# Two-layer encoder on one core: h split ahead of the squares, first three projection groups in three PSUM banks, GpSimd's constants ahead of the bias

## The reference

```python
def rms_norm(x, g):
    xf = x.astype(jnp.float32)
    y = xf * lax.rsqrt(jnp.mean(xf * xf, axis=-1, keepdims=True) + EPS)
    return (y * g.astype(jnp.float32)).astype(x.dtype)

# layer 0: h = rms_norm(x, mix_norm[0]); x = x + neighbourhood_attention(h, ...)
qkv = jnp.einsum('bsd,de->bse', h, w_qkv)       # 1024 -> 3072, 16 heads of 64
s = jnp.einsum('bchd,brckhd->bhcrk', q_r, k_win)
s = s + bias[None]                              # relative bias rpb, gathered by position
p = jax.nn.softmax(s...)
```

## Time and profile before

| | |
|---|---|
| median of three runs | 1189.57 us |
| the profiled execution: its own time, its span | 1191.49 us, 1189.8 us |
| PE busy | 1158.5 us, 97% of the span |
| DVE busy | 644.4 us, 54% |
| ACT busy | 473.6 us, 40% |
| POOL busy | 129.4 us, 11% |
| mean granted TensorE clock | 0.992 |

### The profile page before, as it was taken

How to read it: one execution, slowest core, us unless ns; L and a number is a source line. 1 busy time by engine, 2 the same in 40 slices (tenths; PEclk the granted TensorE clock), 3 DMA queues, 4 the chain that set the end, 5 groups by cost and what they waited for, 6 DMA issues and landing times.

```text
span 1189.8 us, 17258 instructions
## 1 busy us (share of the span) xinstructions
PE 1158.5 (97%) x5940; PEld 953.3 (80%) x5940; DVE 644.4 (54%) x1075; ACT 473.6 (40%) x809; POOL 129.4 (11%) x243
## 2 busy tenths in 40 slices
PE   6899999999999999999999999999999999999995
PEld 4788888877888888888888777787888888888883
DVE  7567677666443224544435888967544233544334
ACT  6444455544342213433233566645443212433221
POOL 4733432050000000000000122100000000000000
PEclk9899999999999999999999999999999999999997
DMA  7322221143222323232232122112222323232321
GB/s 207 99 75 83 68 69 67 51 118 106 94 100 90 103 90 105 88 106 89 88 106 89 50 63 62 33 70 88 93 101 90 105 88 106 88 106 89 106 88 71
DMA packets 35698, 106.74 MB, mean 90 GB/s; under 512 B 8096, under 2 KB 8368, under 8 KB 35664
## 3 DMA queue, kind: packets, MB, share of 16 engines
q1 hardware_dynamic: 30528, 98.98, 25.0%
q0 software_dynamic: 4992, 7.29, 2.8%
q10 hardware_dynamic: 144, 0.02, 0.0%
HBM read 102.92 MB, written 3.34 MB: 89 GB/s over the span
## 4 chain that ended last, share of the span: by engine, by line
PE 92%; DVE 3%; issue 1%; ACT 1%; SPq 1%; POOL 1%; DMA 1%; DVEq 0%; ACTq 0%; POOLq 0%
PE acc L342 26%; PE acc L344 25%; PE acc L343 25%; PE s_ps L342 3%; PE s_ps L343 2%; PE s_ps L344 2%; PE pt_ps L535 2%; PE o_ps L342 1%; PE o_ps L344 1%; PE o_ps L343 1%; PE pt_ps L427 1%; SPq L242 1%; DVE rstd L873 1%; DVE w_lo L851 1%; PE misc_ps L404 1%
## 5 line engine op out<-in xcount | busy, mean ns | idle before, releaser
L632 ACT CAST w_hi<-w_raw 128x1024 fp32r<-128x1024 f32 x180 | 189.1, 1051 | 441.9 <-PE acc L344 430.6
L342 PE MATMUL acc<-h_hi,w_hi 128*128 128x512 f32 x800 | 322.7, 403 | 10.5 <-DVE sqsum L868 9.9
L344 PE MATMUL acc<-h_hi,w_lo 128*128 128x512 f32 x800 | 312.9, 391 | 0.0
L343 PE MATMUL acc<-h_lo,w_hi 128*128 128x512 f32 x800 | 312.8, 391 | 0.0
L851 DVE TENSOR_TENSOR w_lo<-w_raw,w_hi 128x1024 fp32r<-128x1024 f32 x180 | 220.2, 1223 | 147.7 <-ACT w_hi L632 147.6
L342 PE MATMUL acc<-u_hi,w_hi 128*128 128x512 f32 x608 | 238.2, 392 | 0.9 <-DVE w_lo L851 0.9
L344 PE MATMUL acc<-u_hi,w_lo 128*128 128x512 f32 x608 | 236.7, 389 | 0.0
L343 PE MATMUL acc<-u_lo,w_hi 128*128 128x512 f32 x608 | 236.6, 389 | 0.0
L342 PEld LDWEIGHTS acc<-h_hi,w_hi 128*128 128x128 f32 x800 | 150.9, 189 | 50.7 <-issue 17.3
L344 PEld LDWEIGHTS acc<-h_hi,w_lo 128*128 128x128 f32 x800 | 151.0, 189 | 32.0
L343 PEld LDWEIGHTS acc<-h_lo,w_hi 128*128 128x128 f32 x800 | 151.3, 189 | 29.0 <-issue 1.0
(11 more groups left out here) (83 smaller groups left out, 1145.8 us busy)
## 6 DMA issues: line engine op xcount, KB each, us to landing
w_raw<-in_wstream SPq DMA_DIRECT2D x180, 512.0 KB, 3.3
bias_pairs<-rpb_shifted POOLq DMA_DIRECT2D x64, 48.0 KB, 3.1
bias_pairs<-t_shifted POOLq DMA_DIRECT2D x64, 48.0 KB, 2.5
x_res<-in_xT SPq DMA_DIRECT2D x8, 256.0 KB, 4.5
out_y<-x_res SPq DMA_DIRECT2D x8, 256.0 KB, 2.1
t_shifted<-vT POOLq DMA_DIRECT2D x16, 31.0 KB, 1.8
rpb_shifted<-rpb_pad POOLq DMA_DIRECT2D x8, 45.0 KB, 5.2
rpb_shifted<-rpb_pad SPq DMA_DIRECT2D x8, 45.0 KB, 8.1
```

What stands on the lines that cost most here:

```text
L342: nc.tensor.matmul(dst, a[0], b[0], start=start, stop=False)
L343: nc.tensor.matmul(dst, a[0], b[1], start=False, stop=False)
L344: return nc.tensor.matmul(dst, a[1], b[0], start=False, stop=stop)
L632: nc.scalar.copy(w_hi[:, c.odd, :], w_raw[:, c.odd, :]).then_inc(w_hi_made, 1)
```

## The change

ACT and DVE make all eight pieces of h first, and the squares and their sums after them (`first_high`, `first_low`, `first_square`, `first_sum`). PE does groups 0, 1 and 2 in acc0, acc1 and half of `pt_ps`, with `statistics` between groups 1 and 2 (`first_tiles`), so none of the three waits for a bank to be taken out. DVE takes all three results after the reciprocal, and chunk 3 is split ahead of it. On POOL the loads of `sink`, `table` and `onehot_sb` stand before the stores of the bias, and the load of the second pair's bias stands behind the masking of the first pair's. Of the 16 stores SP issues 4 instead of 8, POOL 12 instead of 8.

```diff
@@ SP
-            for c in range(0, QC, 2):
+            for c in range(0, QC, 4):
                 sp.dma_start(rpb_dram[c], rpb_pad[:, :, QC - 1 - c:QC - 1 - c + BIASC]).then_inc(rpb_stored, 16)
@@ POOL
             pool.dma_start(mask[:], na_mask).then_inc(consts_landed, 16)
+            pool.dma_start(sink[:], sinks.partition_broadcast(P)).then_inc(consts_landed, 16)
+            pool.dma_start(table[:], rel_table).then_inc(table_landed, 16)
+            pool.dma_start(onehot_sb[:], onehot).then_inc(table_landed, 16)
             pool.wait_ge(rpb_landed, 16)
-            for c in range(1, QC, 2):
+            for c in range(QC):
+                if c % 4 == 0:
+                    continue
...
             load_na_bias(At(0))
-            load_na_bias(At(1))
-            pool.dma_start(sink[:], sinks.partition_broadcast(P)).then_inc(consts_landed, 16)
-            pool.dma_start(table[:], rel_table).then_inc(table_landed, 16)
-            pool.dma_start(onehot_sb[:], onehot).then_inc(table_landed, 16)
             pool.wait_ge(consts_landed, 16 * 2)
             masked_bias(At(0), 0)
             masked_bias(At(0), 1)
+            load_na_bias(At(1))
@@ PE
+            def first_tiles():
+                for n in range(3):
+                    pe.wait_ge(w_split, CH_NA + n + 1)
+                    bank = acc[n][:] if n < 2 else first_v
+                    for k in ALL:
+                        if n == 0:
+                            pe.wait_ge(first_split, k + 1)
+                        b = slice(k * P, (k + 1) * P)
+                        ins = product(bank, (w_hi[:, n % 2, b], w_lo[:, n % 2, b]), h_tile(k), k == 0, k == KT - 1)
+                    ins.then_inc(w_used, 1)
+                    if n == 1:
+                        statistics(0)
@@ ACT
             for k in range(KT):
-                prepare_x(0, At(k), lambda: act.wait_ge(x_landed[k], 16))
+                first_high(k)
                 if k == 5:
                     split_weights(At(1))
-            na_step(At(0), attend=False)
+            for k in range(KT):
+                first_square(k)
+                if k == 5:
+                    split_weights(At(2))
+            load_sqrt()
+            split_weights(At(3))
+            deviation(0)
+            tile_high(At(GR_NA), At(TI_NA), u_hi[:, 8, :], order=(in_tiles, by_tile))
+            tile_high(At(GR_NA + 1), At(TI_NA + 1), k_hi[:, 0, :], order=(by_column, tokens))
+            split_weights(At(4))
@@ DVE
             for k in range(KT):
-                finish_x(0, At(k))
+                first_low(k)
                 if k == 5:
                     split_weights(At(1))
-            na_step(At(0), attend=False)
+            for k in range(KT):
+                first_sum(k)
+                if k == 5:
+                    split_weights(At(2))
+            split_weights(At(3))
+            reciprocal_deviation(0)
+            scale_tile(At(CH_NA), At(GR_NA), At(TI_NA), HD ** -0.5)
+            scale_tile(At(CH_NA + 1), At(GR_NA + 1), At(TI_NA + 1), 1.0)
+            tile_low(At(TI_NA), u_lo[:, 8, :], u_hi[:, 8, :], (in_tiles, by_tile))
+            tile_low(At(TI_NA + 1), k_lo[:, 0, :], k_hi[:, 0, :], (by_column, tokens))
+            dve.wait_ge(w_used, CH_NA + 3)
+            nc.vector.scalar_tensor_tensor(out=by_column(vT[:, :]), in0=tokens(flat(pt_ps[:, 0:QT, :])), scalar=1.0,
+                                           in1=tokens(rstd[:]), op0=ALU.mult, op1=ALU.mult).then_inc(acc_taken, 1)
+            split_weights(At(4))
```

More of the change, by code:

```diff
@@ L165, in encoder @@
         squared, tile_hi, tile_split = sem("squared"), sem("tile_hi"), sem("tile_split")
+        first_hi, first_split = sem("first_hi"), sem("first_split")
         x_prepared, h_split, sq_cleared = sem("x_prepared"), sem("h_split"), sem("sq_cleared")
@@ L300, in place_sinks @@
                 nc.gpsimd.tensor_copy(sw_nsink[:, pair.odd, :], nsink[:, heads]).then_inc(sinks_placed, 1)
-            pool.wait_ge(rpb_stored, 16 * QC // 2)
-            pool.wait_ge(rpb_stored_odd, 16 * QC // 2)
+            pool.wait_ge(rpb_stored, 16 * QC // 4)
+            pool.wait_ge(rpb_stored_odd, 16 * QC // 4 * 3)
             load_na_bias(At(0))
-            load_na_bias(At(1))
-            pool.dma_start(sink[:], sinks.partition_broadcast(P)).then_inc(consts_landed, 16)
-            pool.dma_start(table[:], rel_table).then_inc(table_landed, 16)
-            pool.dma_start(onehot_sb[:], onehot).then_inc(table_landed, 16)
             pool.wait_ge(consts_landed, 16 * 2)
@@ L392, in statistics @@
                 nc.tensor.matmul(flat(misc_ps[:]), ones[:], sqsum[:], start=True, stop=True).then_inc(stat_done, 1)
+            first_v = flat(pt_ps[:, 0:QT, :])
+            def first_tiles():
[10 more added lines that the diff above has]
+                        statistics(0)
             def part_after_norm(c, g, n):
@@ L458, in dense_part @@
                 def dense_part(n):
-                    if dense and m.a == 0 and n == 0:
-                        part_after_norm(c, g, 0)
-                    elif dense:
+                    if dense:
                         part(c + n, g + n, h_tile, ALL)
@@ L587, in _ @@
             pe.wait_ge(ident_made, 1)
-            na_step(At(0), attend=False)
+            first_tiles()
             na_step(At(1))
@@ L644, in prepare_x, with first_high, first_square @@
                                      ACT.Square).then_inc(x_prepared, 1)
+            def first_high(k):
+                act.wait_ge(x_landed[k], 16)
+                act.wait_ge(gain_landed, 16)
+                nc.scalar.activation(h_hi[:, k, :], x[:, k, :], ACT.Copy, scale=gain[:, k:k + 1]).then_inc(first_hi, 1)
+            def first_square(k):
+                if k >= 2:
+                    act.wait_ge(h_split, k - 1)
+                nc.scalar.activation(probs[:, SEQ * (k % 2):SEQ * (k % 2 + 1)], x[:, k, :],
+                                     ACT.Square).then_inc(x_prepared, 1)
             def gain_of(n, k):
@@ L703, in na_step @@
                 if dense:
-                    if m.a == 0:
-                        load_sqrt()
-                        deviation(0)
                     split_weights(c + 2)
@@ L868, in finish_x, with first_low, first_sum @@
                 nc.vector.tensor_tensor(sqsum[:], sqsum[:], probs[:, SEQ * k.odd:SEQ * (k.odd + 1)],
+                                        ALU.add).then_inc(h_split, 1)
+            def first_low(k):
+                dve.wait_ge(first_hi, k + 1)
+                nc.vector.scalar_tensor_tensor(out=h_lo[:, k, :], in0=x[:, k, :], scalar=gain[:, k:k + 1],
+                                               in1=f32(h_hi[:, k, :]), op0=ALU.mult,
+                                               op1=ALU.subtract).then_inc(first_split, 1)
+            def first_sum(k):
+                dve.wait_ge(x_prepared, k + 1)
+                if k == 0:
+                    dve.wait_ge(sq_cleared, 1)
+                else:
+                    dve.wait_ge(h_split, k)
+                nc.vector.tensor_tensor(sqsum[:], sqsum[:], probs[:, SEQ * (k % 2):SEQ * (k % 2 + 1)],
                                         ALU.add).then_inc(h_split, 1)
@@ L943, in na_step @@
                 if dense:
-                    if m.a == 0:
-                        reciprocal_deviation(0)
                     e = m * 2 + TI_NA
```

## The result

The changed kernel takes 1191.19 us, the median of 20 runs (1189.04 to 1197.02), against 1188.58 for the kernel before, measured beside it (20 runs, 1186.42 to 1192.34). The ratio is 1.0024, with a 95% interval of 1.0015 to 1.0034. A gain of 4.3 us was forecast, and it is 2.6 us slower, outside the range that I gave.

A forecast was written before the change was run, and what follows sets the result against it. PE's 3.86 us idle before the transposes, from POOL's order and SP's queue, was taken as the bound. Transposes 1.0 us earlier plus 3.3 us of clock loss not repeated gave 4.3: 1189.57 to 1185.3 us, range 1180.5 to 1189.5.

The forecast's parts named there:

- The three constants: POOL's front: issuing these loads takes 0.57 us each of 3.18 us idle before the stores, so costs nothing.
- I put it at 20, against a need at 21.4: Front: chunk 3, requested at about 13 behind four SP stores, lands at 20, before its split is needed at 21.4.
- rival C: Front: DVE's chain ends 3 to 4 us late, as when chunk 3 lands after 21.4; 1189.5 us, chance 0.1.
- Rival D: POOL's queue: stores crawl, last lands at 33; 1195 us; decides only from a last store past 30.5; chance 0.05.
- The clock: PE: the clock falls in the new 3.2 us idle at 27.6, losing 3.3 us there instead of later.
- Case B: The forecast itself: PE's clock falls in the new idle; gain 4.3 us, 1185.3 us, chance 0.5.
- The base: Whole kernel: gain reckoned against the profiled 1191.49 us, then taken from the median of 1189.57, including 3.3 us not lost again.
- case A: PE: the clock holds in the new idle ahead of the scores; gain 7.4 us, 1182.2 us, chance 0.35.
- The bias: POOL and SP: last store lands at 19.5, masking done at 29.4, or 31.1 with the latest store, ahead of need.
- The rule of the Trainium skill that I weighed: Bias stores: all issuers share 16 engines, so the last store stays at 22.4; mask at 32.6, still before 33.1.

The follow-up runs named there:

- e10: The changed kernel again, unaltered, for a second profile: 1192.81 us, ratio 1.0025 to before.
- e3: The changed kernel with the loads of sink, table and onehot issued behind POOL's stores: 1189.82 us, ratio 0.9997 to before.
- e2: The changed kernel's new front with POOL and SP as in the kernel before: 1192.09 us, ratio 1.0022 to before.
- e6: The changed kernel with only the load of sink moved behind the stores: 1190.34 us, ratio 1.0015 to before.
- e12: e6 with a stand-in load, 128 rows of 64 bytes from different places, where the changed kernel loads sink: 1191.28 us, ratio 1.0018 to before.
- e5: e3 with chunk 3's split moved behind the values' scaling on DVE and two rounded tiles on ACT: 1187.32 us, ratio 0.9984 to before.
- e11: The changed kernel with a second load of sink right behind the first: 1192.84 us, ratio 1.0031 to before.
- e9: The kernel before with the load of sink alone moved ahead of the stores: 1190.69 us, ratio 1.0005 to before.
- e1: The front of before with the changed kernel's whole POOL and SP part, constants first: 1187.70 us, ratio 0.9981 to before.
- e4: The front of before with the changed POOL and SP part, but constants behind the stores: 1186.48 us, ratio 0.9970 to before.
- e7: e4 with the stores divided as before, eight by SP and eight by POOL: 1186.78 us, ratio 0.9983 to before.
- e8: e5 with four squares and sums between h's pieces, chunk 2 split after sums, statistics inside group 1, chunk 3 split before values' scaling: 1184.85 us, ratio 0.9974.

## Why the prediction was wrong

- **"The three constants take 0.57 each of the 3.18 us that POOL idles before the stores, so nothing."** This step failed first. I priced the issue on POOL and not the transfer on the engines that x is using. `sink`, 8 KB, delays x by 2.4 (k = 3) to 3.1 us (k = 7). In the new front all eight sums stand behind the last piece of x, and that carried 3.0 to the last sum, 2.9 to the reciprocal and 3.2 to the scores.
- **"I put it at 20, against a need at 21.4" (chunk 3).** It landed at 23.0 in the profile of after, 25.2 in e10, 23.5 in e3. This is rival C's mechanism, to which I gave 0.1. In the profile of after it is hidden behind the late x (ACT reaches the split at 24.26); in e2, e3, e6 and e12 it is waited for. The first error covers this one, which is why mending the first alone (e3, e6, e12) brings the scores only 1.2 to 2.7 us forward where x comes 2.8 to 3.1 earlier. I had the row of one chunk that was requested at another time, not what lay ahead of this one: four stores of SP and twelve of POOL. In e3 SP's last store landed at 18.4, and this is what the DMA engines did from 17 to 19 us:

```profile
DMA packets 158, 0.15 MB, mean 75 GB/s; under 512 B 110, under 2 KB 110, under 8 KB 158
q0 software_dynamic: 85, 0.14, 102.1%
```

POOL's stores filled all 16 engines at 75 GB/s, their packets of 2880 B taking 0.7 us each against 0.12 at 12 us, and the chunk's first packet moved at 19.2. That these stores hold the chunk up is what the trace suggests; no run takes them away. Rival D named the same crawl, but the last store landed at 21.4 to 24.0 and not at 33.

- **What was right.** e5 has x nearly on time (13.2) and no wait for chunk 3, so it is the kernel that I had added up. Its reciprocal starts at 24.22 (23.6 put), PE idles 2.49 (3.2), the scores start at 31.44 (30.8), the transposes at 41.05 (41.8). Its span is 4.2 shorter than that of the profiled before, where I had 4.3. Yet its ratio says 1.9 us and its medians 1.0. By the ratios, then, the constants cost some 3.2 us (after to e3) and chunk 3 some 1.5 (e3 to e5), and 2.4 are left for the base and the clock. Each of these is uncertain by one to two microseconds, so that of chunk 3 rests on the traces; and e6 and e12, where x is on time as well, are only 1.1 and 0.7 us ahead of after.
- **The clock.** I had one fall of some 6.6 us in the new idle, no fall after it. The falls were 3.4 (after, e5, e11) and 6.8 us (e2, e6, e10, e12), and 10.2 in e3. Case B's mechanism was right. But the fall differs from run to run, and I had read its size from one. The mean granted clock is on record for 116 runs of before: in the 26 at 0.991 or less the median time is 1192.4, in the 19 at 0.995 it is 1187.1. The 20 runs of after have a median clock of 0.991, those of before 0.993, and 0.002 of the span is 2.4 us of lost work, about the loss that was measured (the clocks are given to 0.001, so this is rough). The kernels with the longer idles of PE between 20 and 100 us (before, after, e2, e3, e6, e9 to e12: 2.9 to 6.1) spread by 4.5 to 8.1 us, those with the shorter (e1, e4, e5, e7: 0.5 to 2.5) by 1.2 to 3.1, and e8 by 4.3, through two runs of 1188.4 and 1188.7 at a clock of 0.991. The 3.5 us up to which rival D takes an idle as harmless is borne out by no run: the clock fell behind idles of 2.49 (e5) and 2.92 (after).
- **The base.** I worked out the gain against an execution of 1191.49 at a clock of 0.992, in which the clock was down for 6.8 us in the stall. The typical run of before is at 0.993 and about 1188.6, so it loses less. Of the 3.3 us that I counted as given back, a part was not there to be had. e4 removes the idle altogether and gains 3.3 us in all by the medians, against 7.4 of case A; its profile has a fall of 3.4 us near 18 us.
- **The bias.** The last store landed at 21.6 (19.5 put, 21.2 as the bound), masking began at 28.34, and the logits did not wait for it in after. The step was right in kind. With x on time the bias is close to binding: in e3, e6 and e12 DVE waited 0.8 for it.
- The rule of the Trainium skill that I weighed (DMA: Bandwidth & Descriptors, "Issuing engines are not separate DMA queues") was put to the stores, where it changes nothing: with 12 and 4 of them the last landed at 21.4 to 24.0, with 8 and 8 at 21.7 to 23.1. It speaks to the constants: POOL's load and SP's loads of x run on the same 16 engines. The traces agree that a load of POOL's can hold up SP's, 256 against 364 GB/s. Why 8 KB cost 0.54 MB it doesn't say.

## What to carry to other kernels

A small load is not free because its issue is: ask what else the DMA engines carry in the microseconds before it lands, and do not put a broadcast of one short row beside the loads of data that everything waits for; behind them it cost nothing here. When work is moved ahead of the step that ends a critical chain, price the arrival of its operands too, since one late weight chunk ahead of a root held the whole front, and price the buffer that it needs. When the medians differ by less than one fall of the clock costs, take the base from many runs and their clocks, and look at more than one profile.

## What I had not expected of the hardware

- A load of 8 KB that reads the same 64 bytes 128 times held the DMA engines so that x landed 2.4 to 3.1 us later. The same shape from 128 different places (e12) did not: 12.5 against 15.7. Nor did the same load behind the stores of e6, where its packets took 0.027 us instead of up to 1.71.
- A store from POOL moves as 16 packets of 2880 B. These took 0.12 us each at 12 us and 0.7 from 15 to 19 us (e3), with SP's small packets beside them and, at 18 us, nearly without. The cause is open.
- In e9 one of DVE's small scalings took 3.16 us where 64 of them have a median of 0.34. It began at 42.3 and ended just after POOL's four maskings (42.52 to 45.30). The rows of e9, by line and on POOL:

```profile
L933 DVE TENSOR_SCALAR probs<-probs,rden x64: 334/343/3162, 41.5 to 235.2; 128x256 f32<-128x256 f32 x64
```

```profile
42.52 2.78 POOL L284 TENSOR_TENSOR bias_masked<-bias_pairs,mask 128x256 f32<-128x256 f32 x4
```

It held the transposes until 45.51 and added some 2.8 us to the idle of PE in that run. The Trainium skill (SBUF — State Buffer, "SBUF: two separate sides") describes a pair of ports that VectorE, in some of its operations, and GpSimd share: whichever takes it first keeps it for a whole instruction, and the other stands still. The coincidence in time fits that, though here DVE stood for four of POOL's instructions and not one. That POOL's work is the cause was not tested.
